# 32 of 48 modulation blocks moved from TensorE rows to sums of products on VectorE, beside the first SwiGLU

## What is computed

```python
def swiglu(h, w_gate, w_up, w_down):
    return (jax.nn.silu(h @ w_gate) * (h @ w_up)) @ w_down
...
    silu_c = jax.nn.silu(c)
    silu_cc = jax.nn.silu(c_ctx)
    for l in range(DEPTH):
        shift, scale, gate = jnp.split(silu_c @ w_mod[l] + b_mod[l], 3, axis=-1)
        shift_c, scale_c, gate_c = jnp.split(silu_cc @ w_mod[l] + b_mod[l], 3, axis=-1)
        hx = _rmsnorm(x, norm_g[l]) * (1.0 + scale[:, None, :]) + shift[:, None, :]
```

## Time and profile before

| | us |
|---|---|
| median of 3 runs | 2503.16 |
| lowest and highest | 2501.81, 2505.79 |
| the profiled execution, its own time | 2502.29 |
| its span, first to last instruction | 2501.0 |
| PE busy | 2357.0 (94%) |
| ACT busy | 863.1 (35%) |
| DVE busy | 835.9 (33%) |
| POOL busy | 680.4 (27%) |
| mean granted TensorE clock | 0.980 |

### The profile page before, as it was taken

How to read it: one execution, slowest core, us unless ns; L and a number is a source line. 1 busy time by engine, 2 the same in 40 slices (tenths; PEclk the granted TensorE clock), 3 DMA queues, 4 the chain that set the end, 5 groups by cost and what they waited for, 6 DMA issues and landing times.

```text
span 2501.0 us, 31188 instructions
## 1 busy us (share of the span) xinstructions
PE 2357.0 (94%) x13320; PEld 1831.1 (73%) x13320; DVE 835.9 (33%) x1358; ACT 863.1 (35%) x1336; POOL 680.4 (27%) x288
## 2 busy tenths in 40 slices
PE   8999999999999999999899999989998989798898
PEld 6766778886888898887667777867874658685566
DVE  5643223202122222223142223035106662512662
ACT  5433233214133343433343322133226332324531
POOL 3122344443332323320323334432210002231001
PEclk9999999999999999999999999999999998999899
DMA  3122332222221212123233333222110001321001
GB/s 117 43 77 84 126 127 94 97 96 82 93 74 67 71 65 76 61 68 102 93 110 127 126 126 110 93 90 96 59 55 9 1 1 43 110 85 55 1 1 68
DMA packets 53290, 192.32 MB, mean 77 GB/s; under 512 B 6688, under 2 KB 7968, under 8 KB 52256
## 3 DMA queue, kind: packets, MB, share of 16 engines
q1 hardware_dynamic: 48960, 178.43, 21.4%
q10 hardware_dynamic: 4192, 11.90, 1.3%
HBM read 188.20 MB, written 2.10 MB: 76 GB/s over the span
## 4 chain that ended last, share of the span: by engine, by line
PE 81%; DVE 6%; ACT 3%; issue 2%; DMA 1%; DVEq 1%; ACTq 0%; POOL 0%
PE ps L182 19%; PE ps L184 19%; PE ps L183 19%; PE ps L185 3%; PE ps L186 3%; PE ps L187 3%; PE ps L2117 2%; PE ps L2143 2%; PE ps L1027 2%; PE ps L1052 2%; PE ps L507 2%; PE ps L2127 2%; PE ps L1037 1%; PE ps L1763 1%; DVE sq L2185 1%
## 5 line engine op out<-in xcount | busy, mean ns | idle before, releaser
L237 POOL TENSOR_TENSOR w_lo<-w_raw,w_hi 128x1024 fp32r<-128x1024 f32 x284 | 680.2, 2397 | 1797.9 <-ACT w_hi L176 1797.7
L176 ACT ACTIVATE w_hi<-w_raw 128x1024 fp32r<-128x1024 f32 x284 | 299.4, 1057 | 622.9 <-DMA w_raw<-in_wstream 621.4
L182 PE MATMUL ps<-h_hi,w_hi 128*128 128x512 f32 x1168 | 472.3, 404 | 18.8 <-POOL w_lo L237 10.7
L184 PE MATMUL ps<-h_hi,w_lo 128*128 128x512 f32 x1168 | 464.8, 398 | 0.0
L183 PE MATMUL ps<-h_lo,w_hi 128*128 128x512 f32 x1168 | 462.4, 396 | 0.0
L182 PEld LDWEIGHTS ps<-h_hi,w_hi 128*128 128x128 f32 x1168 | 220.0, 188 | 100.1 <-issue 26.0
L184 PEld LDWEIGHTS ps<-h_hi,w_lo 128*128 128x128 f32 x1168 | 219.9, 188 | 51.2
L183 PEld LDWEIGHTS ps<-h_lo,w_hi 128*128 128x128 f32 x1168 | 220.2, 188 | 49.7
L1225 ACT ACTIVATE sq<-sq,dnm 128x768 f32<-128x768 f32 x64 | 59.4, 930 | 193.8 <-DVE dnm L1129 193.8
L182 PE MATMUL ps<-l_h_hi,w_hi 128*128 128x512 f32 (+3 forms) x352 | 126.1, 358 | 0.0
L184 PE MATMUL ps<-l_h_hi,w_lo 128*128 128x512 f32 (+3 forms) x352 | 124.1, 353 | 0.0
(11 more groups left out here) (285 smaller groups left out, 3947.2 us busy)
## 6 DMA issues: line engine op xcount, KB each, us to landing
w_raw<-in_wstream SPq DMA_DIRECT2D x332, 512.0 KB, 3.5
l_dft<-in_dft ACTq DMA_DIRECT2D x4, 1024.0 KB, 6.2
x<-in_x SPq DMA_DIRECT2D x4, 512.0 KB, 6.7
out<-x SPq DMA_DIRECT2D x1, 2048.0 KB, 6.3
l_wuq<-in_wuq ACTq DMA_DIRECT2D x2, 768.0 KB, 6.1
dist<-in_dist ACTq DMA_DIRECT2D x1, 1152.0 KB, 5.1
y<-in_ctx ACTq DMA_DIRECT2D x1, 1024.0 KB, 5.6
l_wukv<-in_wukv ACTq DMA_DIRECT2D x2, 512.0 KB, 3.5
```

Of the source, the lines that this page charges most:

```text
L176: self.A.activation(self.w_hi[:, n % RING, :], self.w_raw[:, n % RING, :], ACT.Copy).then_inc(self.w_high, 1)
L182: T.matmul(out, wh, ah, start=start, stop=False)
L184: return T.matmul(out, wl, ah, start=False, stop=stop)
L237: G.tensor_tensor(c.w_lo[:, n % RING, :], c.w_raw[:, n % RING, :], c.w_hi[:, n % RING, :].bitcast(F32), ALU.subtract).then_inc(c.w_low, 1)
```

## The change

The 32 modulation blocks of the two SwiGLUs leave the weight stream (it has 300 blocks then, 16 of them modulation blocks). Their outputs are instead 32 blocks of sums of products on DVE, all in the first SwiGLU and its down blocks:

- The weights come transposed, so that partition p holds the 1024 weights of output p (`wmod`, 512 KB per block). SP issues them on its own queue, ahead of stream block n0+2i+4 for row block i = 0 to 20, then ahead of n0+46 to n0+56, into two buffers of their own; from i = 2 on it first waits for `mod_rows_done` of i - 1 blocks.
- The two conditions come spread over all partitions (1 MB) into `y`, ahead of stream block 8, and ACT takes their Silu in step 0 of the first SwiGLU.
- DVE runs two `tensor_tensor_reduce` per block, one per condition, after `m_lo` of steps 1 to 21; the other 11 blocks follow after the last step.
- The context load waits for all 32.

```diff
-F0_MODS = [(0, 3), (0, 4), (0, 5)]
-F1_MODS = [(1, 1), (1, 2), (1, 3), (1, 4), (1, 5)]
+VECTOR_MODS = [(0, t) for t in range(12, 24)] + [(1, t) for t in range(4, 24)]
...
-def sync_stream(c):
+def sync_stream(c, mods):
     S, w = c.S, c.io["wstream"]
     for n in range(1, NB):
+        if n in mods.at:
+            mods.sync(n)
         if n >= RING:
             S.wait_ge(c.w_used, n + 1 - RING)
         S.dma_start(c.w_raw[:, n % RING, :], w[n]).then_inc(c.landed[n % RING], 16)
...
         if j == 0:
+            A.wait_ge(self.mods.done, self.mods.count)
             A.dma_start(c.y[:, :, :], c.io["ctx"]).then_inc(c.d_y, 16)
...
+class VectorMods:
+    def __init__(self, c, n_cond, at):
+        self.c, self.n_cond = c, n_cond
+        self.count = len(VECTOR_MODS)
+        self.at = {n_cond: None}
+        self.at.update({n: i for i, n in enumerate(at)})
+        assert len(self.at) == self.count + 1
+        self.rows = c.ctx("mod_rows", [P, 2, D_MODEL])
+        self.cond = c.y[:, :, :].rearrange("p k n -> p (k n)")
+        self.products = c.sq[:, :, :].rearrange("p a n -> p (a n)")[:, 0:D_MODEL]
...
+        self.done = c.nc.alloc_semaphore("mod_rows_done")
+
+    def sync(self, n):
+
+        c, i = self.c, self.at[n]
+        if n == self.n_cond:
+            c.S.dma_start(self.cond, c.io["cond"]).then_inc(self.d_cond, 16)
+            return
+        if i >= 2:
+            c.S.wait_ge(self.done, i - 1)
+        c.S.dma_start(self.rows[:, i % 2, :], c.io["wmod"][i]).then_inc(self.d_rows[i % 2], 16)
+
+    def scalar(self):
+        c = self.c
+        c.A.wait_ge(self.d_cond, 16)
+        c.A.activation(self.cond, self.cond, ACT.Silu).then_inc(self.spread, 1)
+
+    def vector(self, i):
+        c, (l, t) = self.c, VECTOR_MODS[i]
+        V = c.V
+        if i == 0:
+            V.wait_ge(self.spread, 1)
+        V.wait_ge(self.d_rows[i % 2], 16 * (i // 2 + 1))
+        for a in range(2):
+            if i or a:
+                V.drain()
+            ins = V.tensor_tensor_reduce(self.products, self.rows[:, i % 2, :], self.cond[:, a * D_MODEL:(a + 1) * D_MODEL],
+                                         1.0, 0.0, ALU.mult, ALU.add, c.modsum[:, l, t, a:a + 1])
+        ins.then_inc(self.done, 1)
...
+        self.first = [n0 + 2 * j for j in range(FT)]
+        self.mods = None
+        if rides:
+
+            self.mods = VectorMods(c, 8, [n0 + 2 * i + 4 for i in range(FT - 1)] +
+                                   [n0 + 2 * FT + 2 + i for i in range(len(VECTOR_MODS) - FT + 1)])
...
-            if self.rides(j) and j % 4 == 3:
-                self.mods.vector(j // 4)
+            if self.mods and j >= 1:
+                self.mods.vector(j - 1)
...
+            if self.mods and j == 0:
+                self.mods.scalar()
...
+    def vector_rest(self):
+
+        for i in range(FT - 1, self.mods.count):
+            self.mods.vector(i)
...
-    f0 = SwiGlu(c, n, "f0", h, F0_MODS, False)
-    n += 2 * FT + 4 * len(F0_MODS)
+    f0 = SwiGlu(c, n, "f0", h, True, None)
+    n += 2 * FT
...
-    f1 = SwiGlu(c, n, "f1", h, F1_MODS, True)
-    n += 2 * FT + 4 * len(F1_MODS)
+    f1 = SwiGlu(c, n, "f1", h, False, f0.mods)
+    n += 2 * FT
...
     f0.vector()
+    f0.vector_rest()
     f0_out.vector()
```

More of the change, by code:

```diff
@@ L51, in dilated_order, with feed_forward @@
     return first, segments
-F0_MODS = [(0, 3), (0, 4), (0, 5)]
-F1_MODS = [(1, 1), (1, 2), (1, 3), (1, 4), (1, 5)]
-def feed_forward(i, mods):
+VECTOR_MODS = [(0, t) for t in range(12, 24)] + [(1, t) for t in range(4, 24)]
+def feed_forward(i):
     s = []
     for j in range(FT):
-        if j < 4 * len(mods):
-            s += [("modrow", *mods[j // 4], j % 4)]
         s += [("gate", i, j), ("up", i, j)]
@@ L72, in stream_plan @@
     s += [("oa", t) for t in range(KT)]
-    s += feed_forward(0, F0_MODS)
+    s += feed_forward(0)
     first, segments = dilated_order()
@@ L76, in stream_plan @@
     s += [("ob", t) for t in range(KT)]
-    s += feed_forward(1, F1_MODS)
+    s += feed_forward(1)
     for l in range(2):
@@ L81, in stream_plan @@
         s += [("out", l, t) for t in range(KT)]
-    assert sorted(b[1:] for b in s if b[0] == "modrow") == [(l, g, q) for l in range(2) for g in range(6) for q in range(4)]
+    on_pe = {(b[1], 4 * b[2] + t) for b in s if b[0] == "modrow" for t in range(4)}
+    assert sorted(on_pe | set(VECTOR_MODS)) == [(l, t) for l in range(2) for t in range(MT)]
     return s
@@ L1255, with __init__ @@
 class ContextNorm:
-    def __init__(self, c):
-        self.c = c
+    def __init__(self, c, mods):
+        self.c, self.mods = c, mods
         self.sq0, self.ss0, self.ad0 = c.squared.take(KT), c.summed.take(1), c.sq_added.take(KT - 1)
@@ L1293, in scalar, with __init__ @@
             A.activation(rb, c.flat(0, 0, CTX), ACT.Sqrt, bias=EPS, scale=1.0 / D_MODEL).then_inc(c.rooted.h, 1)
+class VectorMods:
[8 more added lines that the diff above has]
+        self.products = c.sq[:, :, :].rearrange("p a n -> p (a n)")[:, 0:D_MODEL]
+        self.d_cond, self.spread = c.nc.alloc_semaphore("d_cond"), c.nc.alloc_semaphore("cond_silued")
+        self.d_rows = [c.nc.alloc_semaphore(f"d_mod_rows{i}") for i in range(2)]
+        self.done = c.nc.alloc_semaphore("mod_rows_done")
[23 more added lines that the diff above has]
+        ins.then_inc(self.done, 1)
 class SwiGlu:
-    def __init__(self, c, n0, name, h, mods, context):
-        self.c, self.n0, self.h, self.groups = c, n0, h, len(mods)
-        self.context = ContextNorm(c) if context else None
+    def __init__(self, c, n0, name, h, rides, context):
+        self.c, self.n0, self.h, self.rides = c, n0, h, rides
+        self.context = ContextNorm(c, context) if context else None
         self.mh = c.ctx(name + "m_hi", [P, FT * SEQ], F32R)
@@ L1322, in tensor @@
         for j in range(FT):
[L1323 to L1326, removed]
+            n = self.first[j]
             T.wait_ge(c.w_low, LOWS[n + 1])
@@ L1334, in tensor @@
             c.feat_chunk(n + 1, c.ps[:, 3 + 2 * (j % 2), :], h, range(KT)).then_inc(c.w_used, 1)
-            if self.rides(j) and q == 3:
-                self.mods.tensor_turn(group)
             if self.context and j == KT + 1:
@@ L1343, in vector @@
         for j in range(FT):
-            i, n, cols = j % 2, self.first[j] + self.rides(j), slice(j * SEQ, (j + 1) * SEQ)
+            i, n, cols = j % 2, self.first[j], slice(j * SEQ, (j + 1) * SEQ)
             gr, ur = self.gr[i][:, :], self.ur[i][:, :]
@@ L1365, in scalar @@
         for j in range(FT):
-            i, n, group = j % 2, self.first[j], j // 4
+            i, n = j % 2, self.first[j]
             c.split_high(n + LEAD)
[L1368 to L1372, removed]
+            if self.mods and j == 0:
+                self.mods.scalar()
             A.wait_ge(self.g_out, j + 1)
@@ L1384, in begin @@
             self.c.T.wait_ge(self.c.inverted.h, self.context.rs0 + 1)
-        self.mods.free_banks()
     def late(self):
@@ L2280, in build @@
     begin.sync()
-    sync_stream(c)
+    sync_stream(c, f0.mods)
     S.wait_ge(c.x_added.h, c.x_added.n)
@@ L2425, in lay_out @@
         blocks.append(b)
-    arr = {"wstream": np.stack(blocks)}
+    arr = {"wstream": np.stack(blocks), "wmod": np.stack([g["w_mod_2"][l][:, t * P:(t + 1) * P].T for l, t in VECTOR_MODS]),
+           "cond": np.broadcast_to(np.concatenate([g["c_2"][0].reshape(-1), g["c_ctx_2"].reshape(-1)])[None, :], (P, 2 * D_MODEL))}
     ft = lambda a: a.reshape(-1, P).T
```

## The result

The changed kernel takes 2516.2 us (median of 8 runs, 2512.2 to 2518.3) against 2506.9 for the kernel before (8 runs, 2501.8 to 2511.1): ratio 1.0042, 95% interval 1.003 to 1.0055. It is slower, by 9.4 us between the medians.

The account below looks back on a forecast made before the run. PE, busy 94% of the span and 81% of the chain, was taken to bound the kernel. 2502.3 - 42.1 off PE + 66.5 delay from the DMA-and-sums loop = 2526.7, say 2527 us; own range 2508 to 2545.

Parts of the forecast that it names:

- What leaves PE: Both SwiGLUs: 32 modulation blocks at 1.205 us and 8 transpose turns at 0.435 leave PE's path, 42.1 us off.
- A sum: 1.22 + 0.08 us alone: DVE, first SwiGLU: one 128x1024 sum of products takes 1.22 us plus 0.08 for the accumulator read, 2.6 us a block.
- Rival 3: DVE's sums run at half rate, 2.29 us each, making a loop turn 16.6 us: 2571 us; chance 0.08.
- The sums are shut out by POOL: First SwiGLU: DVE's sums, both operands in SBUF, wait while POOL makes w_lo; one of two lasts about 3.6 us.
- Rival 1: First SwiGLU: POOL does not shut out the sums, only older two-SBUF operations; loop turn 12.2 us, 2479 us; chance 0.12.
- The first round: First SwiGLU, start of the loop: the second sum ends 8.3 us after the up block, releasing SP's wait late.
- The round of 14.5 us: First SwiGLU: loop from sums through SP, DMA, ACT copy, m_hi and m_lo to sums takes 14.5 us against 11.20.
- the same formula: Delay to stream block n0+47 in the first SwiGLU: 8.3 + 20 x 14.5 + 9.0 - 240.8 = 66.5 us.
- The conditions ahead of stream block 8: Window attention: 1 MB more ahead of that block may push one unit's exp 1.5 us; taken as nothing, at most 1.5.
- Rival 2: First SwiGLU: the loop stays below 11.20 us, so only what leaves PE counts: 2460 us; chance 0.14.
- The profile's signs: First SwiGLU: steps near 11.2 us, then 14.5 from about the fifth; PE waits some 3.3 us a step for w_lo.
- the cover of 7.8 us: First SwiGLU: A is ready 7.8 us before PE needs it, so PE is untouched until about the fourth step.

Follow-up runs that it names:

- the PSUM kernel: Against the changed kernel, ACT also copies the conditions to four PSUM banks, where the sums of the first 19 blocks read them: 2476.3 us, ratio 0.989.
- the kernel with the later rows: Against the changed kernel, SP issues row block i ahead of stream block n0+2i+5, not n0+2i+4, and the last eleven two blocks later: 2461.6 us, ratio 0.9825.

## Why the prediction was right, and where its size was off

The direction and the mechanism were right, and 2516.2 lies in the forecast's own range of 2508 to 2545. The size was off: forecast +24 us (2526.7 against 2502.3), measured +9.4 between the medians, less than half of it. The step that was off is the length of a round, which the sum takes twenty times.

- **What leaves PE, 42.1 us.** Right: 43 us without any sums, interval 40 to 50; steps of 11.20 in the first SwiGLU and 11.22 on average in the second.
- **A sum: 1.22 + 0.08 us alone.** Right to 0.01 (1.22 measured, for the sizes it was read from). Rival 3, half rate, is out. The rule of the Trainium skill (Vector Engine (DVE) Microarchitecture Reference, Points that are easy to get wrong) on two non-bf16 SBUF sources is stated there for scalar-tensor-tensor operations; it does not show in this summing one, which takes 1.22 us with two SBUF operands and the same 1.22 with one in PSUM.
- **The sums are shut out by POOL.** Right: 3.37 us beside w_lo in the first round and 3.2 in most later ones, where the sign said about 3.6, and 1.22 with one operand in PSUM. The port rule of the Trainium skill (SBUF — State Buffer, SBUF: two separate sides) agrees: whoever came first kept the other out, in both directions. Rival 1 is out as the cause; the PSUM kernel is nearly its case.
- **The first round, 8.3 us after the up block.** 256.34 - 248.33 = 8.0 (the up block's end is put 0.07 ahead of its evacuation, as in the prediction).
- **The round of 14.5 us.** This is the term that was mis-sized: it measured 13.81, the mean of 19 rounds. About half of the difference is the landing of rows and A, taken as 5.4 us from the earlier trace rows, where the second DMA had been issued about 1 us behind the first. Here they leave 0.37 apart and A is copied after 5.04 on average, 0.36 less. By the spacing of the earlier trace rows it would have been 4.8, the lower bound of the range; the mean lies between the two rows. The other 0.3 us are starts that the prediction counted in full and that passed beside the operation before them: POOL's w_lo of B ends 2.25 us after m_lo and not 2.40, and the accumulator read of the first sum (0.08) delays nothing. That the range's round of 13.8, made by shortening the landing alone, is the measured one is partly luck.
- **The sum.** Put 8.0, 13.8 and 8.4 (A ready at 278.7, 8.4 after 270.35) into the same formula: 8.0 + 20 x 13.8 + 8.4 - 240.8 = 51.6, and 51.6 - 42.1 = 9.5 us slower. The medians say 9.4. The delay alone can be had from the ratios too: 55 us, against 51.6. A round is multiplied by twenty, so 0.7 us of it were 14 us of the forecast's 15 too many. That 9.5 meets 9.4 so closely is luck: the formula misses two things, of opposite sign. The twentieth round lasted only 11.75 us (SP issued rows at 518.75 and 530.50), since one stream block and not two goes out behind those rows and both sums took 1.2; PE began stream block n0+47 at 538.99, 49.9 us late. And the down blocks were not free of further delay: by their end the changed kernel was 54.6 us behind the one without sums (425.7 us from the first gate evacuation against 371.1), with PE's mean granted clock at 0.96 in this last part, against 1.00.
- **The conditions ahead of stream block 8: nothing.** No shift of PE shows in the window attention; the softmax units run 0.2 us earlier than before throughout.
- **Rival 2, the round below 11.20.** Out for the change; 2460 us is what the kernel with the later rows gives (2461.6).
- **The profile's signs.** The steps were 13.8 from the third on rather than from the fifth, since the gate evacuation shows DVE's lateness, and PE's waits (15 times, 28.6 us in all to 510) came later, the first one at about 305 us, as the cover of 7.8 us had it. They were 1.9 us each where the sign said 3.3: 0.7 of this is the shorter round, and most of the rest, some 7 us of 10 over the 15 waits by the mean clock of 0.97 over 220 us (an estimate), is the clock, which the prediction left out.

## What to carry to other kernels

When a DMA queue that feeds the critical engine also carries transfers that wait for another engine's progress, write down the whole ring from that wait back to itself and compare its length with the period of the work; free busy time of the engines says nothing about it. Once the blocks in hand are used up, every microsecond by which the ring is longer is paid once a step, and moving the waiting issue behind the urgent one (here by a single place, for two buffers as before) took the whole loss away: 2461.6 us, 1.75% under the kernel before. Where two engines lock each other out of SBUF, look for an operand that can lie in PSUM: here it took 38 of 38 sums out of the lock.

## What was not expected

- This ring did not stay at its edge. With one sum, the first eleven steps ran at 11.2 us on average, most of them with no margin at all, and then it tipped within two steps to 12.5 us.
- The granted clock fell to its 1.2 GHz level behind quite short waits of PE (most of them 1.8 to 3.4 us), and not behind each of them: two waits of 1.84 us stand in the dilated attention's opening of the kernel before, at clock 1.00 throughout, and the profiles of three experiments show the same two waits with a fall behind each. The same work took 81.0 to 85.3 us there. Those 4.3 us are nearly half of the change's net 9.4, so a single profile could not have given its size.
